# Moving a kernel's constants, arena and split matmul inputs 320 bytes further up in SBUF

## What is computed

```python
# first block
h = rms_norm(x, norm_mix_g); proj = h @ w_in                 # 1024 x 4936
o_a = diff_attention(...); o_b = dsa_attention(...)          # differential; top-64 sparse
x = x + (g_a * (o_a @ w_branch_a) + g_b * (o_b @ w_branch_b)) @ w_out
x = x + memory_attention(rms_norm(x), rms_norm(mem), ...)
x = x + peer_ffn(rms_norm(x), ...)    # 16384 experts, 8 heads x 16 chosen; u, v are 16384 x 1024
x = rms_norm(x, final_norm_g)
# second block, two layers
for i in range(2):
    h = h + (sb_rwkv_mixer if i == 0 else mla_mixer)(rmsnorm(h), ...)
    h = h + conv_glu(rmsnorm(h), ...)                        # 1024 -> 2 x 2816 -> 1024
    h = h + sigmoid(rmsnorm(h) @ ple_w_gate) * rmsnorm(p[i] @ ple_w_proj)
return rmsnorm(h, final_norm)
```

## The kernel before

| tensor | address | mod 512 |
|---|---|---|
| w_high, w_low | 49280, 57472 | 128 |
| consts | 67104 | 32 |
| side, by_row, small | 75296, 78368, 78400 | 32, 32, 64 |
| every room's arena | 80448 | 64 |
| a_high, a_low of the first room | 168512, 184896 | 64 |
| a_high, a_low and s_high, s_low of the PEER room | 211520, 219712; 211520, 215616 | 64 |
| a_high, a_low of the hybrid room | 206400, 217664 | 64 |
| a_high, a_low of the last room | 152128, 184896 | 64 |

## Time and profile before

### The profile page before, as it was taken

One profiled execution on the slowest core, in us unless ns is written; L12 is line 12 of the kernel. 1 busy time (PEld: TensorE's weight loads), 2 busy tenths in 40 slices (PEclk: granted clock), 3 DMA queues, 4 the chain that ended last, 5 costly groups with the idle time before them and its releaser, 6 DMA issues. The chain is left out here.

```text
span 2021.6 us, 45016 instructions
## 1 busy us (share of the span) xinstructions
PE 1877.1 (93%) x16518; PEld 1800.7 (89%) x16518; DVE 1456.5 (72%) x3046; ACT 1242.6 (61%) x2420; POOL 0.2 (0%) x4
## 2 busy tenths in 40 slices
PE   8998988999999999999999989687999977999997
PEld 8887888999999976899999989587999976899996
DVE  7667667688985479766666667776888678578857
ACT  5454655777776789655555556733665555666555
POOL 0000000000000000000000000000000000000000
PEclk9999999999999999999999999798999989999998
DMA  6533344466655620266666646101665644166562
GB/s 208 158 97 105 118 143 136 132 194 193 179 186 175 186 84 0 84 194 190 196 191 193 193 139 199 52 3 56 184 196 173 192 126 136 34 190 189 176 198 76
DMA packets 102084, 296.06 MB, mean 146 GB/s; under 512 B 9539, under 2 KB 32454, under 8 KB 101830
## 3 DMA queue, kind: packets, MB, share of 16 engines
q1 hardware_dynamic: 101958, 294.35, 47.0%
HBM read 293.26 MB, written 1.05 MB: 146 GB/s over the span
## 5 line engine op out<-in xcount | busy, mean ns | idle before, releaser
L459 DVE TENSOR_TENSOR w_low<-ring,w_high 128x512 fp32r<-128x512 f32 x1102 | 743.2, 685 | 357.1 <-ACT w_high L453 349.2
L503 PE MATMUL bank<-a_high,w_high 128*128 128x256 f32 x3228 | 921.2, 285 | 74.3 <-DVE w_low L459 39.1
L504 PE MATMUL bank<-a_low,w_high 128*128 128x256 f32 x3228 | 907.5, 281 | 0.0
L505 PE MATMUL bank<-a_high,w_low 128*128 128x256 f32 x3228 | 907.4, 281 | 0.0
L453 ACT ACTIVATE w_high<-ring 128x512 fp32r<-128x512 f32 x1102 | 671.4, 624 | 375.3 <-PE bank L505 372.8
L503 PEld LDWEIGHTS bank<-a_high,w_high 128*128 128x128 f32 x3228 | 620.0, 192 | 90.0 <-DVE w_low L459 39.7
L504 PEld LDWEIGHTS bank<-a_low,w_high 128*128 128x128 f32 x3228 | 616.3, 191 | 0.4
L505 PEld LDWEIGHTS bank<-a_high,w_low 128*128 128x128 f32 x3228 | 616.7, 191 | 0.0
L503 PE MATMUL bank<-s_high,w_high 128*128 128x256 f32 x1024 | 283.5, 277 | 2.0 <-DVE s_low L2446 2.0
L504 PE MATMUL bank<-s_low,w_high 128*128 128x256 f32 x1024 | 283.3, 277 | 0.0
L505 PE MATMUL bank<-s_high,w_low 128*128 128x256 f32 x1024 | 283.3, 277 | 0.0
(11 more groups left out here) (368 smaller groups left out, 1867.8 us busy)
## 6 DMA issues: line engine op xcount, KB each, us to landing
ring<-in_stream SPq DMA_DIRECT2D x273, 512.0 KB, 3.7
ring<-in_peer_u SPq DMA_DIRECT2D x128, 512.0 KB, 3.6
ring<-in_peer_v SPq DMA_DIRECT2D x128, 512.0 KB, 3.5
ring<-in_stream SPq DMA_DIRECT2D x32, 256.0 KB, 3.3
ring<-in_stream SPq DMA_DIRECT2D x12, 192.0 KB, 2.7
x<-in_x SPq DMA_DIRECT2D x4, 256.0 KB, 6.3
arena<-in_mem SPq DMA_DIRECT2D x1, 1024.0 KB, 11.0
out<-x SPq DMA_DIRECT2D x4, 256.0 KB, 2.6
```

The costliest lines, as they stand in the source:

```text
L459: self.nc.vector.tensor_tensor(self.cut(h, self.w_low), self.raw(h), self.cut(h, self.w_high.bitcast(F32)), ALU.subtract)\
L503: self.nc.tensor.matmul(to, lh, rh, start=start, stop=False, **more)
L504: self.nc.tensor.matmul(to, lh, rl, start=False, stop=False, **more)
L505: return self.nc.tensor.matmul(to, ll, rh, start=False, stop=stop, **more)
```

## The change

`by_row` (16 bytes, which took 32) becomes the first part of a new tensor `filled` of 88 floats (352 bytes), and this stands before `consts` instead of behind `side`. The arena of the hybrid room becomes 256 floats (1024 bytes) shorter.

```diff
-HYBRID_ROOM = 31488
+HYBRID_ROOM = 31232
...
         self.params = sb("params", [P, N_PARAMS])
+        self.filled = sb("filled", [P, 88])
+        self.by_row = self.filled[:, 0:2 * TT]
         self.consts = sb("consts", [P, len(CONSTS), P])
         self.side = sb("side", [P, 6 * P])
-        self.by_row = sb("by_row", [P, 2 * TT])
         self.small = sb("small", [P, 512])
```

## The result

The changed kernel takes 2075.97 us (median of 4 runs, 2072.4 to 2078.45) against 2028.82 us (4 runs, 2020.91 to 2029.96): ratio 1.0226, 95% interval 1.0187 to 1.0264. It is 47 us slower, far beyond the noise (whether by more than 2% the interval leaves open); 2010 was forecast, with a range of 1985 to 2058.

The account below looks back on a forecast made before the run. The prediction took the number of TensorE matmuls times their pitch as the bound. Ending the long state was to save 19 us, 17 arriving: 2004.6 from the profile, 2011.7 from the median; forecast 2010 us, range 1985 to 2058.

Parts of the forecast that it names:

- What bounds the kernel: Whole span: for most of it, time is the number of TensorE matmuls times their pitch; matmuls busy 93%.
- Parts 1 and 2: `by_row` into `filled` with a shorter arena, and constants and arena at new addresses: each taken as 0 us.
- Part 3: Three-product matmuls: split inputs at 384 instead of 64 modulo 512, weights unmoved, save 19.0 us, of which 17 arrive.
- My reading: Split matmuls: near distance 0 the two reads collide once or twice, giving two states; far away once, ending the long state.
- The price: Three-product matmuls: 16.4 us from long stretches plus 2.6 us from short runs, sum 19.0 us saved, 17 arriving.
- Long state gone: Three-product matmuls: stretches at 117.65 ns pitch, 443.7 us in all, would go at 113.3 ns; chance 0.38.
- the case that all matmuls go slower than the long state: All 12,756 split matmuls at, say, 122 ns: 2114 to 2121 us, left outside the range.
- Rival A: Split matmuls: addresses do nothing, states are drawn anew after each wait; 2020 to 2031, say 2027 us; chance 0.27.
- Rival B: Split matmuls: long state everywhere, 36 us slower, 2058 to 2065 us; chance 0.25 including worse.
- Rival C: Split matmuls: a third, shorter state of about 109 ns, 1955 to 1965 us, or 1985 if only part gain; chance 0.10.
- the state is drawn after each wait: Split matmul stream: after each wait for `w_low` it starts anew and settles after some matmuls into 113.3 or 117.65 ns.

Follow-up runs that it names:

- consts_alone: Changed kernel plus 48 spare floats: constants at their new place, arenas and split inputs again at 64 modulo 512; 2025.86 us, 1.0005 of the kernel before.
- inputs_alone: Against the kernel before, only the split inputs move by 320 bytes, to 384 modulo 512; constants and arenas keep their places; 2076.05 us, ratio 1.0243.
- d208: Split inputs 16 bytes further up than in the kernel before, distance to the weights 208 instead of 192 modulo 256; 2063.90 us, ratio 1.0163.
- in_at_192: Changed kernel with `filled` of 40 instead of 88 floats, so split inputs begin 64 bytes above the split weights; 2058.46 us (one run).

## Why the prediction was wrong

**What bounds the kernel** was read rightly: the growth of the matmuls' busy time (51.6 us) and of the span (51.3 us) agree, and VectorE and ScalarE only idle longer. Counting the matmuls and the pitch, 12,756 and 113.3 or 117.65 ns, was sound as well.

**Parts 1 and 2** (other tensors cost 0) hold: `consts_alone` is at 1.0005, `inputs_alone` has the whole loss with the arena in its old place, and the busy times of VectorE and ScalarE moved by 0.2% and 0.4%. (Part 2 puts the constants at 352 modulo 512; they lie at 384.)

**Part 3 failed**, in the sentence "in bytes modulo 512 the moving operand began 64 behind the stationary one, and now begins 256 away, as far as it can". I took 512 bytes for the repeat, and no row said so. The distance repeats every 256 bytes, so 256 is not as far as it can be but the same as 0, both operands at the same place. My reading ("hit once or twice" near distance 0, and so two states) would at most have given those two states there, or the long one throughout, and not 120 ns. Nor is nearness a good rule: 128, the true farthest, is slow too (118.7 ns), and -64, nearer than that, is the best of all that I ran. The states of before are not the edge of a good region on one side of them, as I supposed when I made `d208`: 16 bytes to either side cost 1.6 to 2.1%.

**The price.** Long state gone, -19 us, was the forecast; a pitch that neither state of before has, 120 ns, came instead. I had bounded the unknown price by the two states I could see, and put the case that all matmuls go slower than the long state (122 ns) outside the range. That was the second mistake: 113.3 and 117.65 ns were measured at one distance, and bound nothing at another. By the prediction's own sum 120 ns would have cost 12,756 x 6.7 ns less the 19 us already paid, 66 us, of which the span shows 51; the clock gave 11 back.

**Rival A** (addresses do nothing) is ruled out by `inputs_alone`, in which only the split inputs move. The Trainium skill's page "SBUF — State Buffer", section "Who interferes with whom", calls TensorE's two read ports, one for the moving operand and one for the weight loads, independent. By the measurement they are not, for these float32r matmuls: with both reads walking, the pitch is 1.6 to 8.3 ns longer (113.3 and 120.0 less 111.7). The section's sentence that I quoted, that TensorE never waits on anyone, stands among rules on the engines against each other, and no run here was made to test that. **Rival B** had the sign, and the wrong state: 2058 to 2065 us were its numbers. Its row was better than I took it for: "tm" at +64 showed near the long state, and `in_at_192`, at +64 too, has 117.65 ns. But with a repeat of 256 bytes +64 is as far from the new distance as -64 is, not on the side away from it. **Rival C**'s shorter state exists only with a moving read that stands still, at 111.7 ns rather than 109. Its 109 came from two loads "with no matmul beside them", and that was a misreading; the profile has one from the first load on:

```profile
594.12 0.38 PE L503 MATMUL bank<-a_high,w_high 128*128 128x256 f32 x1 [1.28 <-DVE w_low L459]
```

**That the state is drawn after each wait** was right for the placement of before, and goes with a good part of its spread: in the trace of before, each of the 32 changes between stretches of 15 or more equal steps has a distance over 130 ns in between. And the span grows with the mean pitch in the five traces at distance 192 modulo 256. In the changed kernel there is nearly nothing to draw. Its 4 runs lie within 6 us.

Open: what in the memory or in the reads repeats with 256 bytes, and why 192 is best. I have no reading that gives all nine distances.

## What to carry to other kernels

When a matmul loads its weights while another streams a 4-byte operand of 256 columns, look at the distance between starts in long undisturbed windows. If it differs from stretch to stretch with the same instructions and clock, the placement of stationary against moving tensors may be worth as much as a 2 to 3% change of the program, in either direction. Then don't reason from one measured distance to another: shift one tensor in steps of 16 to 64 bytes over 256 bytes, one profiled run each, and read the pitch from the profile, which is sharper than the time. And every later change of a tensor's size below the matmul operands can move that distance unnoticed, so pin the operands' places.

## What the runs showed of the hardware

- The pitch of float32r matmuls, 128 x 128 stationary and 256 columns moving, each with its own load, depends on the distance between the two operands' addresses, with a repeat of 256 bytes: 120.0 ns at 0, 117.65 at 64, 118.7 on average at 128, 113.3 or 117.65 at 192; 111.7 ns when the moving read doesn't walk.
- At one placement the stream has two steady pitches at a granted clock of 1.00, 113.3 and 117.65 ns, and keeps one for up to 3053 distances in a row (`peer_v` pass of before). It changed only where a distance over 130 ns lay between (32 times in that trace).
- The 17 runs at 120 ns had a mean granted clock of 0.979, the 51 of before 0.974.
- The 512 float32 matmuls of line L2329 (128 x 128) have a median pitch of 112 ns before and after. Both their operands lie in `hot`, so the change moved both alike; what a distance costs float32 matmuls is not shown.
- Moving both halves of the moving operand by 8 bytes, off a multiple of 16, cost 2.5% of the whole kernel; 16 bytes cost 1.6 to 2.1%. Whether the distance or the start within 16 bytes does it is not parted.
